# Two sets of heads in the first attention stage, and another order of ScalarE's and VectorE's work in the recurrent stage

## The chip, the cores and the metric

The kernel runs on one NeuronCore of a Trainium2 chip. Its engines are TensorE (PE in the profile; PEld is its weight load), VectorE (DVE), ScalarE (ACT), GpSimd (POOL) and SyncE (SP), which issues most of the transfers. The metric is the device time of one execution in microseconds; the time of a kernel is the median of its runs.

## The reference

Two blocks of two layers each run over one sequence of 256 tokens with 1024 channels, in fp32. The first block's layer 0 is a mixer of pooling and attention, its layer 1 a recurrent mixer, each followed by a convolutional feed-forward. The second block (three kinds of attention in each layer) is not touched by the change. Cut to what is:

```python
def pool_attn_mixer(h, w_in, pool_w, pool_scale, q_gain, k_gain, w_out):      # layer 0
    u, q, k, v = jnp.split(h @ w_in, [512, 1024, 1536], axis=-1)
    p = multiscale_pool_minus_identity(u)        # mean over 2, 4, 8, 16 tokens, less u, by 128 columns
    p = einsum('bsgc,gcd->bsgd', p.reshape(B, S, 4, 128), pool_w).reshape(B, S, 512) * pool_scale
    a = moba_attention(q, k, v, q_gain, k_gain)  # 8 heads of 64, head_rms on q and k, causal, slopes
    return jnp.concatenate([p, a], axis=-1) @ w_out

def rglru_mixer(h, w_in, conv_w, conv_b, w_a, b_a, w_x, b_x, lam, w_out):     # layer 1
    gate, xr = jnp.split(h @ w_in, 2, axis=-1)   # 1280 columns each
    xr = causal_dwconv(xr, conv_w, conv_b)       # 4 taps
    xb = xr.reshape(B, S, 10, 128)
    r = sigmoid(einsum('bsnc,ncd->bsnd', xb, w_a) + b_a)
    i = sigmoid(einsum('bsnc,ncd->bsnd', xb, w_x) + b_x)
    log_a = -8.0 * r * softplus(-lam)
    a, b = exp(log_a), sqrt(-expm1(2.0 * log_a)) * (i * xr)
    hs = associative_scan(combine, (a, b))       # h[t] = a[t] * h[t-1] + b[t]
    return (gelu(gate) * hs) @ w_out
```

## The kernel before

**Tiling.** Activations lie with channels on the partitions and the 256 tokens along the free axis. All weights come in units of 128 x 2048 floats (1 MB). SyncE transfers unit n into one of three `raw` slots as soon as unit n-3 is split. ScalarE's `split` copies it, rounded, to `w_hi` (L468), after waiting that unit n-3 has been used by TensorE; VectorE's `split` writes the rest, `raw - w_hi`, to `w_lo` (L937). TensorE multiplies each tile in three passes (`three`, L1595 to L1597: high x high, high x low, low x high), 48 matmuls to a unit. Each engine runs its own written list in order and waits on semaphores. `after(n)` on ScalarE and on VectorE does all splits up to unit n+3, so where it stands in an engine's list decides what waits behind a split.

**Stages.** `pa` (12 units, the pooling and attention mixer), `ffn0` (33), `rg` (15, the recurrent mixer), `ffn1`, then the second block. A stage's RMS norm is not applied ahead: the projection runs on x times gain, and VectorE multiplies the result by the reciprocal root (`scale`, L997).

**`pa`.** Units 0 to 3 are the columns of q and k (q heads 0-3, q heads 4-7, k heads 0-3, k heads 4-7), 4 and 5 are v, 6 and 7 are the pooling's u, 8 to 11 the output projection. ScalarE copies each q or k group (L615) and squares it (L617). When all four are there, `set_stat` sums squares by head on TensorE (L1775), ScalarE takes the root (L641), VectorE the reciprocal, `broadcast` spreads it over the partitions (L1798), and `head_norm` (L1165) scales q and k. `token_values` (L626) writes v. `attention` then runs 8 maps, one a head: scores on TensorE by twos (L1825), slope and row minimum on VectorE (L1180, L1182), exponentials on ScalarE (L671), a transpose on TensorE (L1844), its copy to `pt` on ScalarE (L650), the product with v on TensorE (L1866), and after each four heads the division on VectorE (`outputs`, L1199, L1210) and a transpose of that pair of tiles. Halves of units 6 and 7 are put between the maps 0 to 3 on TensorE (`half_units`). GpSimd's `pooling` starts when both u groups are out. After the attention TensorE applies the four pooling matrices (L1925), ScalarE scales the result (L732) and rounds it to `h_hi` (`to_h`, L715), GpSimd writes `h_lo` (L1519), and the four output units run.

**`rg`.** Five steps of 256 columns. Step k has a gate unit g, a branch unit x and an output unit o, in the order `RG_ORDER`. VectorE scales x's group, ScalarE applies bias and last tap (`branch`, L766), VectorE the other three taps (`conv`, L1323). TensorE's `gates` (L1967) multiplies with the two 128 x 128 block matrices, and waits for `conv`. ScalarE takes tanh of both (L781, L783), then exp (L788) and a second tanh (L790); VectorE combines them (L1332), squares the decay `qk[5]` (L1335) and uses it (L1336); ScalarE takes the root (L796), VectorE multiplies and scans along time (L1341, L1343), multiplies with the gelu of the gate (L1351) and rounds (L1356); GpSimd writes `y_lo`, and `second(k)`, the output unit, can run. At the stage's start `first_unit` (g0) is followed by `normed` (L1642), the sum of squares over channels.

Of the kernel before, what the change touches and what calls it, by code (L numbers as in the profile page):

```python
# [28 lines left out]
P = 128  # L29
S = 256  # L30
# [32 lines left out]

HY_STORED = {6: 8, 7: 11, 8: 12, 9: 9, 10: 10, 11: 6, 12: 7}
# [37 lines left out]
def build(nc, W, XT, CON, CON0, VEC, PW, RW, PE_T, POSR, POSC, LAM, OUT, stages=STAGES):  # L102
# [5 lines left out]
    with ExitStack() as ctx:  # L108
# [69 lines left out]
        def pair(t, j):  # L178
# [12 lines left out]
            rgelu rtx xcv rmm rsig rth rm rsb rgy ryhi ry_ready  # L191
# [46 lines left out]
        def stored(n):  # L238


            for a in ffs:
# [44 lines left out]
        def acc_free(eng, s, j, b):  # L286
# [18 lines left out]
            "pa": dict(groups=8, parts=0, pairs=4, sets=1, maps=8, ogroups=2, opairs=2),  # L305
# [11 lines left out]
        def spread_bank(s, k):  # L317


            return bank[2 + (total(s, "pairs") + k) % 4]  # L320
# [136 lines left out]
        def _(act):  # L457
# [228 lines left out]
            def attention(s, fillers):  # L686
# [22 lines left out]
                if kind(s) == "pa":  # L709
                    for u in uses(s, n):  # L710
                        turn(s, u)

# [4 lines left out]
            def pa(s):  # L717
                ub = B[s]
                norm(s)
                for e in range(4):  # L720
                    after(ub + e)
                    evacuate(s, e, pair(qk, e), set_slot(s, e))
                set_root(s, 0, 64, 4)
                for e in (4, 5):
                    after(ub + e)
                    token_values(s, e, 512 * (e - 4)).then_inc(sems["in_ev"], 1)
                attention(s, {1: ub + 6, 3: ub + 7})
                act.wait_ge(sems["vec_in"], 16)
                for j in range(2):
                    act.wait_ge(sems["pm_done"], j + 1)  # L730
                    for t in range(2):
                        last = nc.scalar.activation(hf[:, 2 * j + t], bank[j][:, t * S:(t + 1) * S], ACT.Copy,  # L732
                                                    scale=v_("pool_scale", 2 * j + t))
# [3 lines left out]
                for p in range(2):  # L737
                    act.wait_ge(sems["pt_ev"], use_no(s, ("pair", p)) + 1)
                    to_h(s, hf, 2 + p)
# [10 lines left out]
            def rg(s):  # L750
# [24 lines left out]
                for k in range(RG_STEPS):  # L775
                    hb = lambda t, c: rgh[:, 16 * k + 8 * t + c:16 * k + 8 * t + c + 1]
                    col = lambda v, t: v[:, 2 * k + t:2 * k + t + 1]

                    act.wait_ge(sems["rmm"], k + 1)
# [6 lines left out]
                    act.wait_ge(sems["rsig"], k + 1)  # L786
                    for t in range(2):
                        nc.scalar.activation(qk[:, 10 + t], qk[:, 4 + t], ACT.Exp, scale=col(cneg, t), bias=col(cneg, t))  # L788
                    for t in range(2):
                        last = nc.scalar.activation(qk[:, 8 + t], qk[:, 4 + t], ACT.Tanh, scale=col(cpos, t),  # L790
                                                    bias=col(cpos, t))
                    last.then_inc(sems["rth"], 1)
# [1506 lines left out]
```

## Time and profile before

| | us |
|---|---|
| median of 3 runs | 1630.66 |
| lowest and highest of them | 1629.74, 1633.18 |
| the profiled execution | 1629.44 |
| its span, first to last instruction | 1627.6 |
| TensorE busy | 1565.2 |
| VectorE busy | 1140.0 |
| ScalarE busy | 908.4 |
| GpSimd busy | 163.2 |

Busy time says how long an engine had an instruction under way; the waits of the engine that the end depends on are what a change of order can take away. Stage `pa` lies at 0 to 120 us of the span, `rg` at about 308 to 419 us. Every time below is in microseconds from the span's start. In a row, the bracket at the end is the idle time of that engine just before the row, and the instruction that ended it.

### The profile page before, as it was taken

How to read it: one execution, taken by the hardware profiler on the slowest of the kernel's cores; microseconds unless marked ns; L12 is line 12 of the kernel's file. 1: busy time of each engine (PE TensorE's matmuls, PEld its weight loads, DVE VectorE, ACT ScalarE, POOL GpSimd, SP SyncE). 2: the span in 40 equal slices, each digit the busy share in tenths (PEclk: the TensorE clock that was granted, in tenths of full speed). 3: DMA queues.
4: the chain of work that ended last, by engine and by line, in shares of the span. 5: the costliest groups of instructions: out<-in, count | busy, mean ns of one | idle time of the engine just before them, and what ended most of it. 6: DMA issues, size and time to landing. Idle time of an engine off the chain costs nothing.

```text
span 1627.6 us, 30223 instructions
## 1 busy us (share of the span) xinstructions
PE 1565.2 (96%) x12828; PEld 1510.4 (93%) x12828; DVE 1140.0 (70%) x1366; ACT 908.4 (56%) x1207; POOL 163.2 (10%) x94
## 2 busy tenths in 40 slices
PE   7889999989999999999999999998999999999998
PEld 7779999988999999788899999998889889999998
DVE  6637877877987787667547876568677647777566
ACT  6437554677656555545564744455645645655444
POOL 0121121101012110000022010010000012010010
PEclk9989999999999999999999999999999999999999
DMA  9334555534446545433335455545433334455552
GB/s 319 108 118 159 207 188 188 175 112 151 159 165 209 194 159 181 153 104 104 104 111 181 152 199 181 193 156 181 156 130 104 104 107 159 152 201 178 194 181 78
DMA packets 38268, 258.73 MB, mean 159 GB/s; under 512 B 4752, under 2 KB 5392, under 8 KB 7568
## 3 DMA queue, kind: packets, MB, share of 16 engines
q1 hardware_dynamic: 37728, 255.33, 45.6%
q10 hardware_dynamic: 432, 1.84, 0.3%
q8 instruction: 83, 1.36, 0.3%
q14 instruction: 25, 0.20, 0.0%
HBM read 256.10 MB, written 1.05 MB: 158 GB/s over the span
## 4 chain that ended last, share of the span: by engine, by line
PE 73%; issue 10%; ACT 8%; DVE 7%; POOL 1%; DMA 1%; SPq 0%; ACTq 0%; POOLq 0%; DVEq 0%
PE bank L1595 22%; PE bank L1597 21%; PE bank L1596 21%; ACT w_hi L468 3%; DVE w_lo L937 3%; PE bank L1866 3%; PE bank L1825 2%; PE bank L1844 2%; PE bank L1775 1%; DVE qk L1323 1%; PE bank L1798 1%; DMA raw<-W 1%; PE bank L1967 1%; POOL y_lo L1519 1%; DVE h_lo L952 1%
## 5 line engine op out<-in xcount | busy, mean ns | idle before, releaser
L1595 PE MATMUL bank<-h_hi,w_hi 128*128 128x256 f32 x2640 | 753.1, 285 | 22.9 <-DVE h_lo L952 14.7
L1597 PE MATMUL bank<-h_hi,w_lo 128*128 128x256 f32 x2640 | 742.5, 281 | 0.0
L1596 PE MATMUL bank<-h_lo,w_hi 128*128 128x256 f32 x2640 | 742.5, 281 | 0.0
L937 DVE TENSOR_TENSOR w_lo<-raw,w_hi 128x2048 fp32r<-128x2048 f32 x238 | 553.9, 2329 | 202.2 <-ACT w_hi L468 201.3
L468 ACT ACTIVATE w_hi<-raw 128x2048 fp32r<-128x2048 f32 x238 | 454.9, 1912 | 276.1 <-PE bank L1597 274.4
L1595 PEld LDWEIGHTS bank<-h_hi,w_hi 128*128 128x128 f32 x2640 | 499.2, 189 | 37.1 <-issue 13.6
L1597 PEld LDWEIGHTS bank<-h_hi,w_lo 128*128 128x128 f32 x2640 | 501.7, 190 | 0.0
L1596 PEld LDWEIGHTS bank<-h_lo,w_hi 128*128 128x128 f32 x2640 | 498.8, 189 | 0.4
L1595 PE MATMUL bank<-y_hi,w_hi 128*128 128x256 f32 x1040 | 295.2, 284 | 4.0 <-POOL y_lo L1519 2.2
L1597 PE MATMUL bank<-y_hi,w_lo 128*128 128x256 f32 x1040 | 291.9, 281 | 0.0
L1596 PE MATMUL bank<-y_lo,w_hi 128*128 128x256 f32 x1040 | 291.9, 281 | 0.0
L1595 PEld LDWEIGHTS bank<-y_hi,w_hi 128*128 128x128 f32 x1040 | 195.9, 188 | 7.9 <-issue 3.0
L1597 PEld LDWEIGHTS bank<-y_hi,w_lo 128*128 128x128 f32 x1040 | 197.1, 190 | 0.0
L1596 PEld LDWEIGHTS bank<-y_lo,w_hi 128*128 128x128 f32 x1040 | 195.7, 188 | 0.2
L1519 POOL TENSOR_TENSOR y_lo<-qk,y_hi 128x512 fp32r<-128x512 f32 x53 | 112.4, 2122 | 812.1 <-ACT y_hi L578 698.1
L1041 DVE SCALAR_TENSOR_TENSOR qk<-bank,vec,qk 128x255 f32<-128x255 f32 (+1 forms) x264 | 115.0, 477 | 41.1 <-ACT qk L552 32.7
L997 DVE TENSOR_TENSOR bank<-bank,rinv_t 128x512 f32<-128x512 f32 (+1 forms) x123 | 84.9, 691 | 33.2 <-PE bank L1597 32.4
L552 ACT ACTIVATE qk<-bank,vec 128x256 f32<-128x256 f32 x88 | 44.7, 558 | 103.8 <-DVE bank L997 103.7
L1866 PE MATMUL bank<-val,pt 128*128 128x64 f32 (+1 forms) x448 | 59.3, 276 | 5.7 <-ACT pt L650 5.4
L1866 PEld LDWEIGHTS bank<-val,pt 128*128 128x128 f32 x448 | 56.0, 195 | 7.9 <-ACT pt L650 7.3
L578 ACT ACTIVATE y_hi<-qk 128x512 fp32r<-128x512 f32 x44 | 27.5, 624 | 62.4 <-PE bank L1597 59.3
L567 ACT ACTIVATE qk<-qk 128x512 f32<-128x512 f32 x44 | 27.9, 633 | 60.5 <-DVE qk L1041 60.1
(219 smaller groups left out, 1332.1 us busy)
## 6 DMA issues: line engine op xcount, KB each, us to landing
raw<-W SPq DMA_DIRECT2D x238, 1024.0 KB, 4.8
wide<-RW ACTq DMA_DIRECT2D x1, 1280.0 KB, 7.3
raw<-W SPq DMA_DIRECT2D x2, 512.0 KB, 5.5
x<-XT SPq DMA_DIRECT2D x4, 256.0 KB, 6.7
OUT<-x SPq DMA_DIRECT2D x4, 256.0 KB, 2.0
wide<-CON SPq DMA_DIRECT2D x1, 768.0 KB, 9.1
val<-PE_T ACTq DMA_DIRECT2D x2, 256.0 KB, 2.6
vec<-VEC SPq DMA_DIRECT2D x1, 390.0 KB, 4.8
```

Of the source, the lines that this page charges most:

```text
L468: nc.scalar.activation(w_hi[:, n0 % NW], raw[:, n0 % NRAW], ACT.Copy).then_inc(sems["hi_done"], 1)
L552: ins = nc.scalar.activation(T[:, t], up[:, t * S:(t + 1) * S], ACT.Identity, bias=b, scale=w)
L937: V.tensor_tensor(w_lo[:, n0 % NW], raw[:, n0 % NRAW], w_hi[:, n0 % NW].bitcast(F32), ALU.subtract)\
L997: return V.tensor_tensor(z, z, rinv.unsqueeze(1).broadcast_to([P, w // S, S]), ALU.mult)\
L1041: return V.scalar_tensor_tensor(out=dst, in0=src, scalar=w, in1=dst, op0=ALU.mult, op1=ALU.add)
L1519: return G.tensor_tensor(dst, src, hi.bitcast(F32), ALU.subtract)
L1595: T.matmul(out, w[0], a[0], start=start, stop=False, **kw)
L1596: T.matmul(out, w[0], a[1], start=False, stop=False, **kw)
L1597: return T.matmul(out, w[1], a[0], start=False, stop=stop, **kw)
L1825: last = T.matmul(b[:, qt * S:(qt + 1) * S], qk[p:p + w, tq, qt * P:(qt + 1) * P], qk[p:p + w, tk], start=a == 0, stop=a == n - 1)
L1844: m = T.transpose(b[:, kt * S + qt * P:kt * S + qt * P + P], src[:, qt * S + kt * P:qt * S + kt * P + P], c_("ident"))
L1866: last = T.matmul(o, pt[:, i % 2, kt * S + qt * P:kt * S + qt * P + P], value(m["v"], kt), start=kt == 0, stop=kt == 1)
```

## The change

In `pa` the units come in the order q heads 0-3, k heads 0-3, q heads 4-7, k heads 4-7, v heads 0-3, u first half, v heads 4-7, u second half (`PA_ORDER`), and the output units in the order 2, 0, 1, 3. The head norm is done in two sets of four heads: statistics of set 0 stand between units 2 and 3 on TensorE, its spread behind unit 3, the statistics of set 1 in the middle of unit 4, its spread behind the first half of unit 5. Scores of heads 0 and 1 follow unit 4. Halves of units 5, 6 and 7 lie between maps 0 to 5. The second v group is written by VectorE. Pooling runs in two halves, each as soon as its u group is there. The pooling matrices and the transpose of the last pair stand in the middle of the first output unit, and the `h_lo` of the stage is written by VectorE in place of GpSimd.

In `rg` the first branch unit starts ahead of `normed`; the splits of a step stand ahead of its tanh on ScalarE and ahead of its combination on VectorE; `branch` and `conv` of the next step stand ahead of root and scan (in step 2 the branch stands between scan and output); the square of the decays is ScalarE's; exp of step k waits until step k-1's scan has been used; the last `y_lo` is VectorE's; and the split of unit o3 on VectorE moves from behind step 3 to behind the last step's combination.

```diff
+PA_ORDER = (0, 2, 1, 3, 4, 6, 5, 7, 10, 8, 9, 11)
@@ ScalarE, pa
-                for e in range(4):
+                for e, t in ((0, 0), (1, 2)):
                     after(ub + e)
-                    evacuate(s, e, pair(qk, e), set_slot(s, e))
-                set_root(s, 0, 64, 4)
-                for e in (4, 5):
-                    after(ub + e)
-                    token_values(s, e, 512 * (e - 4)).then_inc(sems["in_ev"], 1)
-                attention(s, {1: ub + 6, 3: ub + 7})
+                    evacuate(s, e, pair(qk, t), set_slot(s, e))
+                set_root(s, 0, 64, 2)
+                after(ub + 2)
+                evacuate(s, 2, pair(qk, 1), set_slot(s, 2))
+                evacuate(s, 3, pair(qk, 3), set_slot(s, 3))
+                after(ub + 3)
+                set_root(s, 1, 64, 4)
+                token_values(s, 4, 0).then_inc(sems["in_ev"], 1)
+                after(ub + 4)
+                attention(s, {1: ub + 5, 3: ub + 6, 5: ub + 7})
@@ ScalarE, rg
+                    after(at(RG_FILL[k]))
+
                     act.wait_ge(sems["rmm"], k + 1)
...
                     act.wait_ge(sems["rsig"], k + 1)
+                    if k:
+
+                        act.wait_ge(sems["rgy"], k)
...
-                    last.then_inc(sems["rth"], 1)
-                    after(at(RG_FILL[k]))
+                        nc.scalar.activation(qk[:, 8 + t], qk[:, 4 + t], ACT.Tanh, scale=col(cpos, t), bias=col(cpos, t))
+                    act.wait_ge(sems["rexp"], k + 1)
+                    nc.scalar.activation(pair(qk, 6), pair(qk, 5), ACT.Square).then_inc(sems["rth"], 1)
+                    if k in (0, 1, 3):
+
+                        branch(k + 1)
@@ VectorE, pa
+                scale_group(s, 2)
                 set_scale(s, 0)
-                for k in range(4):
-                    head_norm(s, k, (2 * k, 2 * k + 1), (v_("pa_gain", 2 * k), v_("pa_gain", 2 * k + 1)))
-                after(ub + 5)
+                after(ub + 2)
+                scale_group(s, 3)
+                pg = lambda t: v_("pa_gain", t)
+                head_norm(s, 0, (0, 1), (pg(0), pg(1)))
+                head_norm(s, 1, (4, 5), (pg(4), pg(5)))
+                set_scale(s, 1)
+                after(ub + 3)
@@ VectorE, rg
                     dve.wait_ge(sems["rth"], k + 1)
-                    link(V.tensor_tensor(pair(qk, 6), pair(qk, 5), pair(qk, 5), ALU.mult))
...
                 for k in range(RG_STEPS):
+                    if k + 1 < RG_STEPS:
+                        after(at(RG_FILL[k]))
                     gates(k)
-                    after(at(RG_FILL[k]))
...
+                    elif k + 1 < RG_STEPS:
                         branch(k + 1)
                         conv(k + 1)
-                    elif k + 1 < RG_STEPS:
-                        branch(k + 1)
                         scan(k)
-                        conv(k + 1)
                         out(k)
                         gate((2, 3, None, 4)[k])
                     else:
+
+                        after(at("x4"))
                         scan(k)
                         out(k)
+                        last_low()
                         after(at("o3"))
-                    if k + 1 < RG_STEPS:
+                    if k + 2 < RG_STEPS:
                         after(at(f"x{k + 1}"))
@@ TensorE, pa
+                attention(s, fill)
+
+                def pooled():
...
+                for n, j in enumerate((2, 0, 1, 3)):
+                    pe.wait_ge(sems["h2_ready"], 4 * atts.index(s) + n + 1)
+                    onto(s, 0, ub + 8 + n, h_parts(j), n == 0, n == 3, between=None if n else pooled)
```

TensorE at the end of the attention in `pa`, before: the transposes of map 7 and of the last pair (`ot`), the pooling matrices (`wide`) and the first output unit (`h_hi,w_hi`).

```order
L1844 MATMUL bank6<-con,lg 128x128 [waits exp_done,pt_ev]
L1844 MATMUL bank6<-con,lg 128x128 x3
L1866 MATMUL bank3<-val,pt 128x64 [waits pt_ev]
L1866 MATMUL bank3<-val,pt 128x64 x3
L1844 MATMUL bank7<-con,ot 128x128 [waits o_ev,pt_ev]
L1844 MATMUL bank7<-con,ot 128x128 x3
L1925 MATMUL bank0<-wide 128x256 [waits pool_in,pool_p]
L1925 MATMUL bank0<-wide 128x256
L1925 MATMUL bank1<-wide 128x256 x2
L1595 MATMUL bank0<-h_hi,w_hi 128x256 [waits lo_done,h2_ready,psc]
```

The same place in the changed kernel:

```order
L1901 MATMUL bank6<-con,lg 128x128 [waits exp_done,pt_ev]
L1901 MATMUL bank6<-con,lg 128x128 x3
L1929 MATMUL bank3<-val,pt 128x64 [waits pt_ev]
L1929 MATMUL bank3<-val,pt 128x64 x3
L1649 MATMUL bank0<-h_hi,w_hi 128x256 [waits lo_done,h2_ready,in_ev]
```

The output unit follows the last map at once; the transpose of the pair and the pooling matrices stand 24 matmuls further on.

ScalarE in step 0 of `rg`, before: tanh from banks 6 and 7, exp and tanh with scales from `geo`, a split (`w_hi`), root, then `branch` from bank 5.

```order
L781 ACTIVATE qk<-bank6,geo 128x256 [waits rmm,rgc_ready]
L781 ACTIVATE qk<-bank6,geo 128x256
L783 ACTIVATE qk<-bank7,geo 128x256 x2
L788 ACT_TABLE_LOAD
L788 ACTIVATE qk<-qk,geo 128x256 [waits rsig]
L788 ACTIVATE qk<-qk,geo 128x256
L790 ACTIVATE qk<-qk,geo 128x256 x2
L468 ACTIVATE w_hi<-raw 128x2048 [waits w_used,raw_in2]
L796 ACT_TABLE_LOAD
L796 ACTIVATE qk<-qk 128x512 [waits rm]
L766 ACTIVATE qk<-bank5,vec 128x256 [waits scaled]
```

And in the changed kernel:

```order
L472 ACTIVATE w_hi<-raw 128x2048 [waits w_used,raw_in2,rgc_ready]
L790 ACTIVATE qk<-bank6,geo 128x256 [waits rmm]
L790 ACTIVATE qk<-bank6,geo 128x256
L792 ACTIVATE qk<-bank7,geo 128x256 x2
L800 ACT_TABLE_LOAD
L800 ACTIVATE qk<-qk,geo 128x256 [waits rsig]
L800 ACTIVATE qk<-qk,geo 128x256
L804 ACTIVATE qk<-qk,geo 128x256 x2
L806 ACTIVATE qk<-qk 128x512 [waits rexp]
L773 ACTIVATE qk<-bank5,vec 128x256 [waits scaled]
L773 ACTIVATE qk<-bank5,vec 128x256
L812 ACT_TABLE_LOAD
```

The split stands ahead of tanh, the square (L806) is new, and `branch` stands ahead of the root.

VectorE in the last step of `rg`, before: the gate of step 4, a split (`w_lo`, unit o3), the three instructions of the combination, a split (unit o4), the scan.

```order
L1311 TENSOR_TENSOR qk<-bank4,rinv_t 128x512 [waits w_used]
L937 TENSOR_TENSOR w_lo<-raw,w_hi 128x2048 [waits hi_done]
L1332 SCALAR_TENSOR_TENSOR qk<-qk 128x512 [waits rsig]
L1335 TENSOR_TENSOR qk<-qk 128x512 [waits rth,dve_chain]
L1336 SCALAR_TENSOR_TENSOR qk<-qk 128x512 [waits dve_chain]
L937 TENSOR_TENSOR w_lo<-raw,w_hi 128x2048 [waits hi_done]
L1341 TENSOR_TENSOR qk<-qk 128x512 [waits rsb]
L1343 SCALAR_TENSOR_TENSOR qk<-qk 128x256 [waits dve_chain]
```

And in the changed kernel:

```order
L1353 TENSOR_TENSOR qk<-bank4,rinv_t 128x512 [waits w_used]
L1374 SCALAR_TENSOR_TENSOR qk<-qk 128x512 [waits rsig]
L1377 SCALAR_TENSOR_TENSOR qk<-qk 128x512 [waits rth,dve_chain]
L953 TENSOR_TENSOR w_lo<-raw,w_hi 128x2048 [waits hi_done]
L1382 TENSOR_TENSOR qk<-qk 128x512 [waits rsb]
L1384 SCALAR_TENSOR_TENSOR qk<-qk 128x256 [waits dve_chain]
```

The split between combination and scan is now that of unit o3; the split of o4 stands behind the last `y_lo`.

## Rows read from the trace of the kernel before

**Rows 1.** The page: busy time of TensorE.

```profile
PE 1565.2 (96%) x12828; PEld 1510.4 (93%) x12828; DVE 1140.0 (70%) x1366; ACT 908.4 (56%) x1207; POOL 163.2 (10%) x94
```

**Rows 2.** Waits of TensorE, 0 to 125 us: total, times, longest.

```profile
PE bank L1866 <- ACT pt L650: 2.9, 4, 1.3
PE bank L1825 <- ACT val L626: 2.9, 1, 2.9
```

**Rows 3.** TensorE by stretches: length, busy (instructions), granted clock, DMA share, GB/s.

```profile
55.62:58.26 2.64, 2.64 (x12) 0.50 0.60 133
75.25:84.10 8.85, 5.78 (x45) 1.00 0.16 44
84.10:97.67 13.57, 9.55 (x37) 0.62 0.11 48
97.67:120.30 22.63, 22.63 (x191) 1.00 0.39 133
345.60:358.30 12.70, 12.70 (x97) 0.88 0.39 124
```

**Rows 4.** TensorE in order of time, stage pa: start, duration, instruction, count.

```profile
25.61 0.37 PE L1595 MATMUL bank<-h_hi,w_hi 128*128 128x256 f32 x1
...
60.29 1.13 PE L1825 MATMUL bank<-qk 64*128 64x256 f32 x8
...
64.29 1.00 PE L1866 MATMUL bank<-val,pt 128*128 128x64 f32 x8
65.13 0.61 PE L1844 MATMUL bank<-con,lg 128*128 128x128 f32 x4
```

**Rows 5.** ScalarE and VectorE in order of time, stage pa.

```profile
32.13 0.59 ACT L617 ACTIVATE sq<-bank 128x512 f32<-128x512 f32 x1
...
31.76 2.29 DVE L937 TENSOR_TENSOR w_lo<-raw,w_hi 128x2048 fp32r<-128x2048 f32 x1 [0.16 <-ACT w_hi L468]
...
45.55 3.22 DVE L1165 SCALAR_TENSOR_TENSOR qk<-qk,vec,bank 128x256 f32<-128x256 f32 x8 [1.69 <-PE bank L1798]
...
90.94 0.76 DVE L1210 TENSOR_TENSOR ot<-bank,rec 128x256 f32<-128x256 f32 x2
```

**Rows 6.** Waits of TensorE, 300 to 425 us: total, times, longest.

```profile
PE bank L1967 <- DVE qk L1323: 9.0, 4, 3.1
PE bank L1642 <- DVE sq L984: 1.2, 1, 1.2
```

**Rows 7.** TensorE in order of time, stage rg: the gates of steps 0, 1 and 4.

```profile
327.40 1.89 PE L1967 MATMUL bank<-qk,wide 128*128 128x256 f32 x8
...
343.76 2.45 PE L1967 MATMUL bank<-qk,wide 128*128 128x256 f32 x8 [3.10 <-DVE qk L1323]
...
398.53 2.61 PE L1967 MATMUL bank<-qk,wide 128*128 128x256 f32 x8 [2.12 <-DVE qk L1323]
```

**Rows 8.** ScalarE in order of time, step 0 of stage rg.

```profile
329.39 0.84 ACT L781 ACTIVATE qk<-bank,geo 128x256 f32<-128x256 f32 x2 [3.77 <-PE bank L1967]
...
330.97 1.28 ACT L788 ACT_TABLE_LOAD   x1
...
333.27 1.08 ACT L790 ACTIVATE qk<-qk,geo 128x256 f32<-128x256 f32 x2
334.25 1.90 ACT L468 ACTIVATE w_hi<-raw 128x2048 fp32r<-128x2048 f32 x1
...
337.47 0.63 ACT L796 ACTIVATE qk<-qk 128x512 f32<-128x512 f32 x1
339.12 1.02 ACT L766 ACTIVATE qk<-bank,vec 128x256 f32<-128x256 f32 x2 [1.02 <-DVE bank L997]
```

**Rows 9.** VectorE in order of time, steps 0 and 1 of stage rg.

```profile
335.18 0.69 DVE L1336 SCALAR_TENSOR_TENSOR qk<-qk 128x512 f32<-128x512 f32 x1
...
339.71 1.27 DVE L1343 TENSOR_TENSOR_SCAN qk<-qk 128x256 f32<-128x256 f32 x2
341.02 2.69 DVE L1323 SCALAR_TENSOR_TENSOR qk<-bank,vec,qk 128x255 f32<-128x255 f32 x6
```

More of the change, by code:

```diff
@@ L238, in stored @@
         def stored(n):
+            if "pa" in used and B["pa"] <= n < B["pa"] + UNITS["pa"]:
+                return first + B["pa"] + PA_ORDER[n - B["pa"]]
             for a in ffs:
@@ L304, in build @@
         PLAN = {
-            "pa": dict(groups=8, parts=0, pairs=4, sets=1, maps=8, ogroups=2, opairs=2),
+            "pa": dict(groups=8, parts=0, pairs=4, sets=2, maps=8, ogroups=2, opairs=2),
             "hy": dict(groups=30, parts=5, pairs=13, sets=3, maps=24, ogroups=8, opairs=6)}
@@ L736, in pa @@
                     to_h(s, hf, j)
-                for p in range(2):
-                    act.wait_ge(sems["pt_ev"], use_no(s, ("pair", p)) + 1)
-                    to_h(s, hf, 2 + p)
+                act.wait_ge(sems["pt_ev"], use_no(s, ("pair", 1)) + 1)
+                to_h(s, hf, 3)
                 for n in range(8, 11):
@@ L1851, in outputs @@
                 g = total(s, "ogroups") + m["g"]
+                if kind(s) == "pa" and i == 0:
+                    pe.wait_ge(sems["qk_done"], total(s, "pairs") + 4)
+                if kind(s) == "pa" and i == 4:
+                    pe.wait_ge(sems["in_ev"], total(s, "groups") + 7)
                 if kind(s) == "hy" and i == 0:
@@ L1906, in pa @@
                 normed(s)
-                for e in range(2, 4):
-                    feature_unit(s, ub + e, e)
+                feature_unit(s, ub + 2, 2)
+                pe.wait_ge(sems["picked"], 1)
+                set_stat(s, 0, 0, [two(0), two(4)], 1)
+                feature_unit(s, ub + 3, 3)
+                pe.wait_ge(sems["spread_in"], 12 * 16)
+                broadcast(s, 0, 0, [(0, 2), (4, 2)])
                 unit(ub + 4)
@@ L1918, in pa @@
-                pe.wait_ge(sems["qk_done"], total(s, "pairs") + 4)
-                pe.wait_ge(sems["in_ev"], total(s, "groups") + 6)
-                attention(s, half_units(s, ub + 6, 6, 2))
-                pe.wait_ge(sems["pool_p"], 1)
-                pe.wait_ge(sems["pool_in"], 16)
-                for g in range(4):
-                    m = T.matmul(bank[g // 2][:, (g % 2) * S:(g % 2 + 1) * S],
-                                 wide[:, 13:15].rearrange("p a n -> p (a n)")[:, g * P:(g + 1) * P], pool_u[:, g, 8:8 + S],
-                                 start=True, stop=True)
-                    if g % 2:
-                        m.then_inc(sems["pm_done"], 1)
@@ new lines, in pa @@
+                attention(s, fill)
+                def pooled():
+                    pe.wait_ge(sems["o_ev"], total(s, "opairs") + 2)
+                    transposed(s, ("pair", 1))
+                    pe.wait_ge(sems["lp_done"], total(s, "maps") + 8)
+                    pe.wait_ge(sems["pool_p"], 1)
+                    pe.wait_ge(sems["pool_in"], 16)
+                    for g in range(4):
+                        m = T.matmul(bank[4 + g // 2][:, (g % 2) * S:(g % 2 + 1) * S],
+                                     wide[:, 13:15].rearrange("p a n -> p (a n)")[:, g * P:(g + 1) * P], pool_u[:, g, 8:8 + S],
+                                     start=True, stop=True)
+                        if g % 2:
+                            m.then_inc(sems["pm_done"], 1)
```

114 lines of the change are left out of this document (78 added, 36 removed).

## The prediction

> **What bounds the kernel.** I read the page's busy times first, then TensorE's waits by stage, then the engines in order of time around the longest waits. TensorE is busy for 96% of the span [rows 1]. Its work is the same after the change but for one more start of each statistics group, so only its waits, and the stretches in which its granted clock is low, can be won. In stage pa the waits are one of 2.9 us ahead of the scores, four for the copies to `pt` [rows 2], and the tail of the attention, where TensorE idles 8.85 - 5.78 = 3.1 us and then 13.57 - 9.55 = 4.0 us, the second stretch at a mean clock of 0.62 [rows 3]. In stage rg it waits four times for the taps, 9.0 us in all, and once 1.2 us for the sum of squares [rows 6]; after the first of these the clock is 0.88 over two units [rows 3]. A unit takes 22.63 / 4 = 5.7 us at the high level [rows 3], half a unit 2.85.
>
> **Stage pa, first half.** Unit 2 starts at 25.61 [rows 4] and ends at 31.3. The statistics of set 0 now stand right behind it and need the square of group 1, which ends at 32.13 + 0.59 = 32.7 [rows 5]: a new wait of 1.5. From there TensorE runs 0.5 of statistics, unit 3, 0.5 of spread (to 39.7), unit 4 with 0.5 of statistics inside, and is at the scores at 45.9. VectorE's scaling of group 3, four head norms (half of 3.2 us for eight, [rows 5]) and a second reciprocal fit beside unit 4, so the scores don't wait: 2.9 gone. What is late next is the first transpose. VectorE has the split of unit 6 ahead of the logits; 2.3 for the split [rows 5], two instructions of 0.7 like those in [rows 9], then the exponentials behind a split and a table load on ScalarE bring it to 51.2, where TensorE has been free since 50.35: a wait of 0.85. The 2.9 wait was followed by a low clock that I put at 1.4 to 1.8 by a half unit of 24 matmuls (some 14 of them 0.10 longer, the difference of the two levels in [rows 3], and the scores); that goes with it. First half: -2.9 - 1.6 + 1.5 + 0.85 = -2.1.
>
> **Stage pa, tail.** Six half units now cover maps 0 to 5 where four covered 0 to 3. Scores take 1.06, a product 0.84, a transpose 0.45, by the distances of starts and the durations less their overlap [rows 4]. With these TensorE goes without a wait from 51.2 to the end of the transposes behind unit 7 at about 76. Then ScalarE has a split of 1.9 [rows 8] ahead of the copy of map 5, since that split waits for unit 7 to be used: 0.8 of waiting. The last maps are a chain through ScalarE as before: waits of about 0.7, 0.8, 0.2 and 0.8. The last product ends at 83.3, then reciprocal, division (0.76, [rows 5]) and the subtraction for the first `h_lo`, 0.69 as for any two-input pass of 512 [rows 9], lie on the path because VectorE's list has the division first: 1.8 to 2.0 of waiting, and the output units start at 85.0 instead of 97.67 [rows 3]. Pooling in halves ends on GpSimd near 84 and isn't waited for. The transpose of the pair and the pooling matrices (0.5 + 1.6 at the high clock) now lie inside the first output unit, and their copies, roundings and subtractions (about 3 us through ScalarE and VectorE) are covered by its second half of 2.85. I add 0.9, because half units between maps take 2.94 and not 2.85 (4.00 from 60.29 to 64.29 less 1.06) and a waited-for group ends some 0.1 later. So 85.0 + 22.6 + 2.1 + 0.9 = 110.6 without any low clock, against 120.3 [rows 3]. The waits from 76 to 85 sum to 5.1 in 9 us, against 3.1 in 8.85 us that were followed by the 0.62 stretch. So I count on a low clock again, over three to five short groups and the first matmuls of the output units: 1.7 to 3.9, take 2.8. Stage pa ends at 113.4: **-6.9** (-5 to -10).
>
> **Stage rg, start.** The sum of squares waits 1.2 less, but stands behind half a unit more. From it, root, reciprocal, gate, split, scale, `branch` and `conv` take 10.9 us to the first gates, and TensorE has only 2.85 + 5.7 to do meanwhile. The gates of step 0 come at 327.8 against 327.40 [rows 7]: +0.4, two waits (0.5 and 1.0) for one.
>
> **Stage rg, steps.** Before, from tanh at 329.39 the chain ran tanh, load, exp, tanh, then square, combination, split, scale, product, scan (1.27) and at last taps, which end at 343.71 [rows 8, 9]: 14.3. Now: the second tanh starts 3.88 after the first [rows 8], the square 1.0 later for 0.6, combination and scale 1.35 by two steps of 0.61 and a latency, `branch` 1.02 [rows 8], taps 2.69 [rows 9]: 10.7. VectorE loses 0.69 and ScalarE gains 0.6 for the square; one handover is neither gained nor lost. The gates of step 1 then need only the gate unit in front, 340.8 against 343.76 [rows 7]. But ScalarE's own round is now a bound: tanh to square 5.5, wait 1.4, `branch` 1.0, load 1.28 and root 0.6, load and gelu 1.9, two splits 3.8 = 15.5, against 13.0 of TensorE's work in a step with two units. So tanh of step 1 starts at 345.3, of step 2 at 360.8, step 3 at 377.7, though TensorE is ready 2.5, 2.8 and 1.0 earlier. Adding 10.7, the gates start at 340.8, 355.9, 374.8 and 388.4 (steps 1 to 4; step 3 is held by root and scan of step 2, which stand ahead of that branch). TensorE waits 2.2 at step 2, 0.2 at step 3, 0.7 for the split of x4 (now behind the taps), nothing at step 4: before, the last gates came at 398.53 [rows 7], so **-10.1** to that point.
>
> **Stage rg, end.** Here a wait comes back. The split of o3 on VectorE stands behind the last combination. ScalarE does the split of o4, a load (1.28) and then tanh at 392.5; square and combination end at 397.4, the split at 399.65. TensorE has done gates and o2 at 395.6: a wait of **4.05** ahead of o3. Queued behind it is only o4, for which `y` is ready at 403.5 and the split at 405.7. So o3 and o4 end at 411.05 at the high clock, 419.3 before. A wait of 4.05 is longer than that of 3.10 [rows 7] after which 12.70 us passed for 11.4 of work plus 0.5 in the gates [rows 3]: I add 2.0. The 2.2 wait may cost as much, but most of it is swallowed by the 4.05; 0.6 for it. The first unit of ffn1 waits some 0.3 more for its splits. 411.05 + 2.0 + 0.6 + 0.3 = 414.0: **-5.3** (-2 to -8).
>
> **Sum.** -6.9 - 5.3 = -12.2 on 1629.44, 1617.2; the median stood 1.2 above that execution: **1618**. The later stages are the same, but wherever the clock is about to fall or rise there, 2 us may come or go.
>
> **A rule of the Trainium skill against this.** In this trace a table load lasts 1.28 and the next function starts 0.02 behind it; the load at 330.97 is one [rows 8]. The Trainium skill ("ScalarE: Activation LUTs", What ACT_TABLE_LOAD costs) counts a drain of about 1.38 us to each switch, 2.66 in all. By that rule ScalarE's round would have three switches of 1.38 more, and since the changed order makes that round the bound, an estimate by that page would take 12 us back over three rounds, 1630. The row shows no such drain, so the sum keeps 1.28.
>
> **Rivals.** (1) Forecast, 1612 to 1624: **66%**. (2) The waits I see coming back don't: the tail of pa keeps the high clock (-2.8), and the o3 wait with its low clock is short because ScalarE reaches tanh earlier (-4 to -6). For: three of the waits rest on splits placed by a few tenths. Against: the order lists fix o3 behind the combination. 1618 - 8 = 1610; **14%** for 1605 to 1612. (3) Only one stage pays: ScalarE's round slips further (exp now waits for the last output of the step before, splits wait for units), each round 1.7 longer, and rg gives nothing: 1624 to 1627.4; **12%**. (4) No change, within 0.2%: rounds 4 us longer in rg, as if each table switch drained: 1630; **4%**. (5) Slower: TensorE stays at the low level through the four output units of pa because the short waits from 76 to 85 are closer together. At a granted clock of 0.50, the 1.2 GHz level, a matmul takes 2.64 / 12 = 0.22, the first stretch of [rows 3], instead of 0.12; 192 of them cost 19.2 more, 1618 + 19.2 - 2.8 = 1634.4, and with o3 and o4 low too, 96 x 0.10 = 9.6 less the 2.0 counted, 1642. It is slower by over 0.2% from about 190 low matmuls on, o3 and o4 among them; before, the high level was back for the whole of the output units [rows 3]. **4%**.
>
> The time is the forecast's. Low 1609 takes in most of rival 2, high 1625 some of rival 3. A measurement can tell about 0.2%, 3.3 us, from no change: faster 92%, within 4%, slower 4%.
>
> **What would show it.** The scores start near 46 and the output units of pa near 85; gates of step 4 near 388; a wait of about 4 for `w_lo` ahead of the o3 unit, the longest of rg; ScalarE's tanh of steps 1 and 2 starting right behind a split, not behind TensorE. Wrong would be: gates waiting over 3 us for the taps, or no wait at o3.

## The result, and the profile after

| | before | after |
|---|---|---|
| median, us | 1630.66 | 1618.79 |
| lowest and highest, us | 1629.74, 1633.18 (5 runs) | 1614.69, 1622.99 (5 runs) |
| the profiled execution, its span | 1629.44, 1627.6 | 1618.79, 1617.0 |

The ratio is 0.9925, with a 95% interval of 0.9909 to 0.9942. The prediction was 1618.0. Measured a second time, beside eleven runs of the kernel before, the changed kernel had a median of 1616.30 us (1613.03 to 1621.55, 6 runs) against 1629.84: 0.9922, interval 0.9905 to 0.9939.

The page of after answers to [rows 1]: TensorE's busy time hardly moves, and the span gets 10.6 us shorter.

```profile
PE 1563.3 (97%) x12828; PEld 1509.5 (93%) x12828; DVE 1140.0 (71%) x1369; ACT 909.9 (56%) x1211; POOL 157.5 (10%) x91
```

TensorE's waits, 0 to 125 us, and then 300 to 425 us, in after (total, times, longest), answer to [rows 2] and [rows 6]:

```profile
PE bank L1649 <- DVE h_lo L968: 11.1, 2, 9.8
PE bank L1929 <- ACT pt L654: 2.2, 3, 0.8
PE bank L1649 <- issue: 1.7, 1, 1.7
PE bank L1829 <- ACT sq L621: 1.3, 1, 1.3
...
PE bank L1649 <- DVE w_lo L953: 3.5, 1, 3.5
PE bank L2058 <- DVE qk L1365: 2.6, 2, 1.9
PE bank L1649 <- DVE h_lo L968: 1.3, 1, 1.3
```

The 9.8 us are the start of the kernel. The 2.9 us ahead of the scores are gone, and 1.3 for the first set's statistics and 1.7 ahead of the output units have come. The 9.0 us for the taps have become 2.6, and 3.5 ahead of one `w_lo` have come. In order of time, TensorE in after (start, duration, instruction, count, and the wait ahead in the bracket), first stage `pa`, then the gates, o3 and the next feed-forward stage's start in `rg`:

```profile
32.21 1.06 PE L1829 MATMUL bank<-sq,con 128*32 128x256 f32 x8 [1.32 <-ACT sq L621]
39.08 1.13 PE L1852 MATMUL bank<-crs,con 32*128 32x256 f32 x8
43.17 1.06 PE L1829 MATMUL bank<-sq,con 128*32 128x256 f32 x8
47.24 1.13 PE L1882 MATMUL bank<-qk 64*128 64x256 f32 x8
...
88.83 0.55 PE L1649 MATMUL bank<-h_hi,w_hi 128*128 128x256 f32 x1 [1.73 <-issue]
...
116.47 0.36 PE L1649 MATMUL bank<-h_hi,w_hi 128*128 128x256 f32 x1 [1.26 <-DVE h_lo L968]
...
337.90 1.89 PE L2058 MATMUL bank<-qk,wide 128*128 128x256 f32 x8
353.05 2.44 PE L2058 MATMUL bank<-qk,wide 128*128 128x256 f32 x8 [1.89 <-DVE qk L1365]
...
386.57 1.89 PE L2058 MATMUL bank<-qk,wide 128*128 128x256 f32 x8
397.69 0.35 PE L1649 MATMUL bank<-y_hi,w_hi 128*128 128x256 f32 x1 [3.54 <-DVE w_lo L953]
...
412.08 0.35 PE L1649 MATMUL bank<-h_hi,w_hi 128*128 128x256 f32 x1 [1.26 <-DVE h_lo L968]
```

The places to compare are the starts of the first feed-forward stage and of the second. Before, they lie at 121.89 and 420.42. One table of TensorE over three stretches tells how the time between was won: unit 2 of `pa` to the first feed-forward unit, 160 us inside the first feed-forward stage, and the gates of step 0 to the next feed-forward stage. The columns are the stretch, its length, TensorE busy (instructions), granted clock, DMA share, GB/s. Before:

```profile
25.61:121.89 96.28, 84.76 (x658) 0.93 0.42 146
130.00:290.00 160.00, 159.78 (x1380) 1.00 0.56 191
327.40:420.42 93.02, 83.02 (x619) 0.94 0.40 139
```

After:

```profile
24.96:116.47 91.51, 84.55 (x658) 0.94 0.44 153
130.00:290.00 160.00, 159.43 (x1350) 1.00 0.54 184
325.00:412.08 87.08, 80.38 (x617) 0.96 0.41 150
```

Length less busy is waiting. In `pa` it falls from 11.5 to 7.0 us and the busy part stays: 4.8 us in length, and unit 2 itself began 0.65 earlier, so the stage ends 5.4 earlier. (The 0.65 is not the change's: `low_first` below, with the same start, has unit 2 at 25.74.) In `rg` waiting falls from 10.0 to 6.7, and the busy part from 83.0 to 80.4 for the same matmuls: 5.9 us. Before has three stretches of 3.4 us at the 1.2 GHz level there and after two. There a matmul takes 0.215 us from start to start and not 0.117, so the third stretch was worth at most 1.7 of the 2.6 us. Most of the other 0.9 goes with the waits themselves: the first matmul of the gates behind a wait takes 0.32 us to the next one instead of 0.22, and the last one ahead of a wait counts as busy to its end. Between the two lies what nobody forecast: in the same 160 us after starts 1350 matmuls where before starts 1380, at the same granted clock of 1.00. Over the whole stretch from 121.89 to 327.40 and from 116.47 to 325.00 that is 205.5 us against 208.5, and 3.0 us of the gain were given back there. From the second feed-forward stage on, 2.3 us more were won, in a part that the change doesn't touch: -5.4 + 3.0 - 5.9 - 2.3 = -10.6. Before spends 3.4 us more at the 1.2 GHz level there, worth up to 1.7 of the 2.3.

### The profile page after: what moved, and what is told of

Its sections match the earlier page's. It is cut to its first block, busy times and chain, and to the rows that moved or that the text cites. A ratio compares the mean times of both kernels' runs of the same rounds, so it can differ in the third digit from the quotient of the medians.

```text
span 1617.0 us, 30230 instructions
## 1 busy us (share of the span) xinstructions
PE 1563.3 (97%) x12828; PEld 1509.5 (93%) x12828; DVE 1140.0 (71%) x1369; ACT 909.9 (56%) x1211; POOL 157.5 (10%) x91
## 4 chain that ended last, share of the span: by engine, by line
PE 75%; issue 12%; ACT 7%; DVE 5%; POOL 1%; DMA 1%; SPq 0%; POOLq 0%; ACTq 0%; DVEq 0%
PE bank L1649 22%; PE bank L1650 21%; PE bank L1651 21%; ACT w_hi L472 3%; PE bank L1882 2%; PE bank L1929 2%; PE bank L1901 2%; DVE w_lo L953 2%; PE bank L1829 1%; PE bank L1852 1%; DVE rinv_t L1007 1%; DMA raw<-W 1%; POOL y_lo L1571 1%; DVE bank L1013 0%; ACT h_hi L492 0%
## 5 line engine op out<-in xcount | busy, mean ns | idle before, releaser
L571 ACT ACTIVATE qk<-qk 128x512 f32<-128x512 f32 x44 | 27.9, 633 | 60.5 <-DVE qk L1065 60.1
```

## Experiments: the two halves apart

The theory was that two separate gains add up; the rival, that `rg` gains only because `pa` ends earlier. The first kernel has `pa` of after with `rg` of before, the second the reverse. Of the one block that both stages share on GpSimd, each took its own line:

```diff
 # pa_only
-                    for q in range(RG_STEPS - 1):
+                    for q in range(RG_STEPS):
 # rg_only
+                    to_h(s, hf)
```

> The attention stage of the changed kernel with the recurrent stage of the kernel before. Theory (two separate gains): the first feed-forward unit starts 5.4 us earlier than in the kernel before (116.47 against 121.89, as in the trace after), the recurrent stage keeps the length of the kernel before, from the start of its last covered feed-forward units to the start of the next feed-forward stage 8.34 - 2.24 = 6.1 us longer than in the changed kernel; time 1630.7 - 5.4 = 1625 us, and up to 3.6 us more or less by the pace that the matmul stream takes in the first feed-forward stage (0.1156 or 0.1183 us a matmul, 1344 of them). Rival (the recurrent stage gains only because the stage before it ends earlier and its loads come earlier): its waits of 9.0 us at one line shrink here too, time near 1620.

> The attention stage of the kernel before with the recurrent stage of the changed kernel. Theory: the recurrent stage is 6.1 us shorter than in the kernel before, the attention stage unchanged (first feed-forward unit near 121.9); time 1630.7 - 6.1 = 1624.5 us, up to 3.6 us more or less by the pace of the stream in the first feed-forward stage. If the two halves of the change are independent, the two gains add up to the 11.9 us between the medians within that pace term. Rival (the gain of the recurrent stage depends on the other half): less than 4 us shorter.

Measured, ten runs of each beside nineteen of the kernel before (median 1629.97): `pa_only` 1626.10 us, ratio 0.9986 (0.9963 to 1.0008), so its gain is not clear of the spread by time alone; `rg_only` 1623.64, ratio 0.9961 (0.9937 to 0.9985). The two gains add up to 3.9 + 6.3 = 10.2 us, against 11.9 between the medians at first. The times alone don't settle it: the runs of the kernel before reach from 1620.34 to 1638.46 there. The positions in the trace do. The first feed-forward unit starts at 116.97 in `pa_only` and 121.47 in `rg_only`. From the gates of step 0 to the second feed-forward stage, `pa_only`:

```profile
325.93:420.07 94.14, 84.03 (x619) 0.93 0.40 138
```

and `rg_only`:

```profile
326.80:412.68 85.88, 79.17 (x616) 0.98 0.42 152
```

Beside 93.02 before and 87.08 after, each half has its own effect and none of the other's: -4.9 for `pa`, -7.1 for `rg` here. The rival is out. `pa_only` has 3.4 us more at the 1.2 GHz level than before in this stretch, and is 1.1 longer. Five traces have this same `rg` in full, and they show what one trace can say: 87.08 (after), 85.86 (`after_again`), 85.88 (`rg_only`), 85.88 (`stat_mid`), 87.01 (`low_first`). The 1.2 us of after are one stretch at the 1.2 GHz level behind the gates of step 2, which the four others don't show; `low_first` ran twice as long at that level around the start of o3.

## Experiments: what in stage rg gains

Three parts of the change were undone one at a time in the changed kernel. First the splits, behind the gates again on both engines:

```diff
 # ScalarE
-                    after(at(RG_FILL[k]))
-
                     act.wait_ge(sems["rmm"], k + 1)
...
                     nc.scalar.activation(pair(qk, 6), pair(qk, 5), ACT.Square).then_inc(sems["rth"], 1)
+                    after(at(RG_FILL[k]))
 # VectorE
-                    if k + 1 < RG_STEPS:
-                        after(at(RG_FILL[k]))
                     gates(k)
+                    if k + 1 < RG_STEPS:
+                        after(at(RG_FILL[k]))
```

> The changed kernel with another part undone: the splits of a step stand behind its gates again, on ScalarE (3.7 us for two) and on VectorE (5.2 us for two). Theory (the splits inside the chain from tanh to taps were what the waits of 9.0, 4 and 3.1 us of the kernel before came from): the stage gets 5 to 8 us longer than in the changed kernel, with the waits ahead of the gates back at the taps. Rival (ScalarE's round of 15.3 us bounds, wherever the splits stand in it): less than 2 us.

Then the order of the taps:

```diff
 # VectorE
-                        conv(k + 1)
                         scan(k)
+                        conv(k + 1)
                         out(k)
 # VectorE, step 2: branch and conv behind out and the split of o0
 # ScalarE: branch(k + 1) behind the root, in every step
-                    if k in (0, 1, 3):
-
-                        branch(k + 1)
```

> The changed kernel with one part undone: the taps of the next branch behind the scan on VectorE again, and ScalarE's first tap behind the root. Theory by the trace after: in step 0 the taps end 1.4 us later (gates of step 1 about 1.2 later), but ScalarE's round gets 1.3 us shorter, since it no longer waits for VectorE's scaling of the branch ahead of the root, and VectorE's two splits bound the next step: gates of step 2 within 0.5 us of the changed kernel; stage 0 to 2 us longer. Rival (the prediction's view, the chain from tanh to taps of 10.7 against 14.3 us carries the gain): 3 to 6 us longer.

Then the squares of the decays:

```diff
 # VectorE
+                    link(V.tensor_tensor(pair(qk, 6), pair(qk, 5), pair(qk, 5), ALU.mult))
 # ScalarE
-                    nc.scalar.activation(pair(qk, 6), pair(qk, 5), ACT.Square).then_inc(sems["rth"], 1)
```

> The changed kernel with its third part undone: the squares of the decays on VectorE (0.69 us) instead of ScalarE (0.62 us). Theory: the square lies between the second tanh and the gate's product on either engine, so a step changes by 0.1 us; from the first to the last gates within 0.6 us of the 60.4 to 61.6 us that the traces with the square on ScalarE have. Rival (VectorE or ScalarE is full at that point, and the move of 0.6 us counts in every step): 2 to 3 us longer.

The same stretch, gates of step 0 to the second feed-forward stage, in `splits_behind`:

```profile
322.77:416.38 93.61, 83.22 (x616) 0.95 0.39 137
```

in `taps_behind`:

```profile
325.95:410.96 85.01, 78.60 (x617) 1.00 0.42 149
```

in `square_dve`:

```profile
327.15:413.49 86.34, 79.11 (x616) 0.98 0.42 151
```

and in a second trace of the changed kernel itself, `after_again`. It lacks the low stretch of step 2, as `taps_behind` and `square_dve` do, and is the one to compare with:

```profile
322.68:408.54 85.86, 79.09 (x617) 0.98 0.42 152
```

With the splits behind the gates everything is lost: 93.6 us, 0.6 longer than before the change. Undoing the squares costs 0.5 us, less than the traces of one kernel differ by. The order of the taps bought nothing here: undone, the stretch is 0.85 **shorter**, where I expected 0 to 2 us longer. Each of these is one trace; single runs took 1624.08 us (`splits_behind`) and 1615.40 (`taps_behind`) beside 1632.97 for the kernel before, and 1617.74 (`square_dve`) beside 1635.72. The other parts of the change in `rg` (x0 ahead of `normed`, the last `y_lo` on VectorE) were not undone by themselves. My forecast had priced the chain of 10.7 against 14.3 us as one piece, splits and taps together. Two engines in `taps_behind` show what each part does, ScalarE in step 0 and the start of step 1, then VectorE's taps:

```profile
327.95 0.84 ACT L790 ACTIVATE qk<-bank,geo 128x256 f32<-128x256 f32 x2 [0.70 <-PE bank L2054]
...
334.75 0.63 ACT L808 ACTIVATE qk<-qk 128x512 f32<-128x512 f32 x1
335.29 1.00 ACT L773 ACTIVATE qk<-bank,vec 128x256 f32<-128x256 f32 x2
...
342.21 0.84 ACT L790 ACTIVATE qk<-bank,geo 128x256 f32<-128x256 f32 x2 [0.37 <-PE bank L2054]
...
337.44 2.68 DVE L1361 SCALAR_TENSOR_TENSOR qk<-bank,vec,qk 128x255 f32<-128x255 f32 x6
```

and the same of after:

```profile
327.00 0.84 ACT L790 ACTIVATE qk<-bank,geo 128x256 f32<-128x256 f32 x2 [0.69 <-PE bank L2058]
...
333.93 1.02 ACT L773 ACTIVATE qk<-bank,vec 128x256 f32<-128x256 f32 x2 [1.45 <-DVE bank L1013]
...
342.34 0.82 ACT L790 ACTIVATE qk<-bank,geo 128x256 f32<-128x256 f32 x2
...
334.98 2.69 DVE L1365 SCALAR_TENSOR_TENSOR qk<-bank,vec,qk 128x255 f32<-128x255 f32 x6 [1.09 <-ACT qk L773]
```

From tanh to the taps' end the changed kernel needs 337.67 - 327.00 = 10.7 us and `taps_behind` 340.12 - 327.95 = 12.2, so the splits, with the square, take 2.1 us out of the 14.3 and the taps' place 1.5. But in the changed kernel ScalarE idles 1.45 us, waiting for VectorE's scale ahead of the first tap, with the root queued behind; its round is 15.3 us and the next tanh starts with no wait, right behind a split. With the taps behind, the first tap follows the root without that wait, and the round is 14.3, ended by TensorE. Over the first two steps the two are 0.5 us apart. The later steps do cost `taps_behind` more, 62.7 us from first to last gates against 60.5 in `after_again`. That is then taken back ahead of o3, where both wait for the same split on VectorE: 1.71 us there, 3.55 in `after_again`. No low clock follows the 1.71, and one stretch follows the 3.55.

That wait was tried next: in the changed kernel VectorE makes the low half of o3, or of o3 and o4, ahead of the last gates.

```diff
-                    if k + 1 < RG_STEPS:
-                        after(at(RG_FILL[k]))
+                    after(at(RG_FILL[k]) if k + 1 < RG_STEPS else at("x4"))   # o3_early; at("g4") in o34_early
                     gates(k)
...
-                        after(at("x4"))
                         scan(k)
```

> Recurrent stage of the changed kernel, but VectorE makes the low half of unit o3 ahead of the last step's gates, in its idle time of 2.0 us there (389.9 to 391.9). Theory (the 3.54 us wait ahead of o3 is that split, and o4's is the next thing late): o3 starts without a wait near 394.2 instead of 397.7; o4's split still stands behind the last combination and its low half, done near 402.6, so a new wait of about 2.5 us appears ahead of o4; start of the next feed-forward stage 1.5 to 2 us earlier than 412.1 (counted from the same start of the stage). Rival (full gain): no wait ahead of o4, 4 us earlier. Second rival: the last step's gates slip by the split, and nothing is gained.

> As o3_early, but the low halves of both o3 and o4 stand ahead of the last step's gates on VectorE. The two splits take 4.5 us of which 2.0 were idle; the first gate operation slips by 2.4 us, but the second waits for ScalarE's square until 394.65 anyway and slips by 0.3. Theory: no wait ahead of o3, at most 0.5 us ahead of o4 (for the last product's low half, near 400.3), no low-clock stretch there; next feed-forward stage 4 to 5 us earlier than in the changed kernel. Rival: the slip of the gates passes down the chain in full (2.4 us), o4 waits 2.5 us, gain 2 us or less.

> Both splits of o3 and o4 ahead of the last gates on VectorE (as in the run o34_early), and the taps behind the scan again (as in taps_behind). In the changed kernel the later gates of taps_behind (62.7 us from first to last gates against 60.4) were taken back by a shorter wait ahead of o3 (1.71 against 3.54 us). Theory (the taps' order counts only once the wait ahead of o3 no longer hides it): first gates to the next feed-forward stage 81.8 + 2.3 = about 84 us. Rival (the order of the taps is worth nothing in any case): 81.8 to 82.3.

The same stretch, in `o3_early`:

```profile
325.68:409.15 83.47, 77.75 (x616) 1.00 0.42 153
```

in `o34_early`:

```profile
324.23:406.03 81.80, 77.79 (x616) 1.00 0.43 159
```

in `o34_taps_behind`:

```profile
325.74:408.79 83.05, 77.87 (x617) 1.00 0.44 157
```

and VectorE in order of time ahead of the last gates' products in `o34_early`:

```profile
387.88 5.21 DVE L953 TENSOR_TENSOR w_lo<-raw,w_hi 128x2048 fp32r<-128x2048 f32 x2
393.01 0.68 DVE L1374 SCALAR_TENSOR_TENSOR qk<-qk 128x512 f32<-128x512 f32 x1
393.72 0.69 DVE L1377 SCALAR_TENSOR_TENSOR qk<-qk 128x512 f32<-128x512 f32 x1
```

Both splits early are worth 4.1 us beside `after_again`, 5.3 beside the first trace of after: 2.8 us of waiting (6.8 to 4.0) and the rest in the busy part (79.1 to 77.8), which has no stretch at the low level any more. One split moved gives 2.4 beside `after_again` and 3.6 beside after, where I expected 1.5 to 2; a wait of 2.95 comes ahead of o4, where I expected 2.5, but no low clock follows it, and that is what the expectation left out. The theory sized o4's wait in `o34_early` at 0.5 at most and it is 1.2: the two splits took 5.2 us and not 4.5, so the gates' second product came 1.0 us later and not 0.3, and the root 0.5. The first of the two took 3.0 us and not 2.3, with a `y_lo` on GpSimd in its first 0.8 us; the same split takes 3.0 beside a `y_lo` in `o3_early` (389.32) and in after (341.28). Now that nothing hides it, the order of the taps counts: 83.05 - 81.80 = 1.25 us, where I expected 2.3. So the same edit is worth -0.85 or +1.25, by what stands ahead of o3, one trace on each side.

## Experiments: the two new waits of stage pa

```diff
 # low_first, VectorE: ahead of the division of the last group
+                            if kind(s) == "pa" and e == n - 1:
+                                pair_low(s, 0, 2)
                             outputs(s, ended(s, e))
 ...
 # stat_mid, TensorE
-                set_stat(s, 0, 0, [two(0), two(4)], 1)
-                feature_unit(s, ub + 3, 3)
+                unit(ub + 3)
+                b = group_bank(s, 3)
+                column_tile(ub + 3, 0, b[:, 0:S])
+                set_stat(s, 0, 0, [two(0), two(4)], 1)
+                column_tile(ub + 3, 1, b[:, S:2 * S]).then_inc(sems["w_used"], 1)
```

> Attention stage of the changed kernel, but VectorE makes the low half of the first output block (0.68 us, its inputs are there at 85.6) ahead of the division of the last group (0.20 + 0.76 us) instead of behind it. Theory (the 1.73 us wait ahead of the four output units is that order on VectorE): the output units start right behind the last product, 1.7 us earlier; counted from the last product's start to the first feed-forward unit 1.7 us shorter than the 31.34 us of the changed kernel (85.13 to 116.47). Rival: the transposes and pooled matmuls inside the first output unit, which need the division, now wait; gain below 0.5.

> Attention stage of the changed kernel, but the statistics of the first set of heads stand in the middle of unit 3 instead of ahead of it. Theory (the 1.32 us wait is for ScalarE's squares of unit 2, and half a unit covers it): no wait there, and no wait ahead of the spread behind unit 3 or at most 0.5; scores and all that follows 0.8 to 1.3 us earlier, counted from the start of unit 2. Rival (the chain statistics, root, reciprocal, spread, norm, scores is what bounds, and it now begins later): the wait comes back at the spread or ahead of the scores, gain under 0.3, or a loss of up to 1.5.

> The changed kernel with three edits together: the splits of o3 and o4 ahead of the last gates on VectorE, the low half of the first output block ahead of the division, the statistics in the middle of unit 3. Theory: the stretch from the first gates to the next feed-forward stage is 81.8 us (87.1 in the changed kernel), the attention stage 1.7 + 1.0 us shorter; 8 us less than the changed kernel of the same chip, near 1611 us, with runs spread by some 14 us in steps of 3.6 us, one for each of the four feed-forward stages that takes the slower pace. Rival (the spread comes from elsewhere): the runs lie within 0.3% of their median.

> The changed kernel itself, beside the one with three edits and the kernel before on one chip. Theory: ratio to before 0.9925 as first measured, within its interval (11 us: 5.4 from the attention stage, 5.9 from the recurrent stage, less 3.2 where its first feed-forward stage took the slower pace, which must not happen in every run, so possibly up to 13). Rival: the first measurement drew lucky paces, ratio above 0.995.

From unit 2 to the first feed-forward unit, in `low_first`:

```profile
25.74:114.81 89.07, 83.86 (x659) 0.96 0.45 156
```

in `stat_mid`:

```profile
24.93:116.36 91.43, 85.80 (x658) 0.93 0.45 153
```

in `after_again`:

```profile
25.25:116.97 91.72, 84.75 (x659) 0.94 0.44 153
```

and in `best`:

```profile
25.59:110.94 85.35, 81.26 (x659) 1.00 0.47 165
```

Waiting falls from 7.0 us in `after_again` to 5.2 with the low half first and to 5.6 with the statistics in the middle. Both waits go in full and come back nowhere. From the last product to the first feed-forward unit `low_first` takes 29.8 us, against 31.3 after: 1.5 of the 1.7 expected. In `stat_mid` the scores start 45.82 - 24.93 = 20.9 us behind unit 2, against 22.3 after, a little more than the 0.8 to 1.3 expected. But `stat_mid` is only 0.3 us shorter, for its tail ran at the low level 3.4 us longer. The four rows differ by 4.5 us in the busy part for the same matmuls, and `best`, whose tail never fell, shows the price: at most 84.75 - 81.26 = 3.5 us for the 10.2 us at the low level in `after_again` (at most, since `best` has two waits less there, and these leave the busy part a little too). With the same edits apart it fell in every trace, so I don't claim that they prevent it together. No run undoes a part of the first change in `pa` by itself; that its 4.8 us come from the 2.9 ahead of the scores and from the covered maps is read from the waits alone.

`best` has these two edits and that of `o34_early`. Five runs gave 1608.19 us (1605.62 to 1611.88), ratio to before 0.9868 (0.9849 to 0.9886): 8.1 us less than the changed kernel measured beside it, as expected. Its `rg` stretch was 82.66, against 81.8 expected. The spread that I expected of its runs, 14 us, was 6.3, within 0.3% of the median to either side, so on `best` the rival's expectation held; the spread shows in other runs (below).

## Why the prediction was right, and where it wasn't

The time was right within 0.8 us. Part of that is luck: -6.9 - 5.3 had to become -5.4, +3.0, -5.9 and -2.3.

**Stage pa, first half.** Unit 2 to scores was to take 20.3 us and took 22.3. The failed step is a term: I wrote 0.5 us for a group of eight short matmuls, twice for statistics and once for the spread. From start to start they take 33.20 - 32.21 = 0.99 and 40.14 - 39.08 = 1.06. The halves of unit 4 took 3.0 to 3.1 and not 2.85. The new wait was 1.32 against 1.5, and the one of 0.85 ahead of the first transpose never came: TensorE was late itself.

**Stage pa, tail.** The chain through ScalarE waited 0.82, 0.45, 0.69 and 0.69 us against 0.8, 0.7, 0.2 and 0.8, and the wait behind VectorE's division was 1.73 against 1.8 to 2.0; `low_first` shows its cause. The pooled matmuls lay inside the first output unit as said. The low clock came and cost some 3.3 (84.55 - 81.26, at most) against 2.8. Output units started at 88.83 against 85.0: 1.3 was there at the scores, 0.7 came by the transposes behind unit 7 (77.9 against 76), and 1.9 in the last maps, where the clock fell at 81.4. In `o34_early`, where it fell only at 87.4, the same maps took 78.6 to 87.5, 8.9 us, as the 9.0 in the forecast. So the order was right there; the sum added the whole low clock only behind the 85.0.

**Stage rg, steps.** Counted from the gates of step 0, I had those of steps 1 to 4 at 13.0, 28.1, 47.0 and 60.6 us. After has them at 12.9, 28.1, 48.5 and 61.6, the extra low stretch among it, `after_again` at 13.2, 28.1, 46.7 and 60.5. ScalarE's round was 15.3 against 15.5. A table load in it lasts 1.28 us and the next function follows 0.02 behind, as in [rows 8]:

```profile
328.58 1.28 ACT L800 ACT_TABLE_LOAD   x1
329.88 1.09 ACT L800 ACTIVATE qk<-qk,geo 128x256 f32<-128x256 f32 x2
```

These rows show no drain, and rival 4, rounds 4 us longer, is out. The Trainium skill ("ScalarE: Activation LUTs", What ACT_TABLE_LOAD costs) counts a drain of about 1.38 us to each switch of function set, by an estimate from that figure 4.1 us for the three of a round; this trace does not agree, and the measurement decides.

What was wrong here is the account of what buys what, and not the number. The chain came out at the 10.7 us of the forecast (whose listed terms add up to 10.5), but the sum took it as one piece and ScalarE's round as its given limit. The round is that long **because of** the taps' order, which puts ScalarE's wait for VectorE's scale ahead of the root: 15.3 us against 14.3 without it. So the order takes 1.5 us out of the chain and puts 1.0 into the round. The splits ahead of the gates carry the gain, 7.8 us beside `after_again`.

**Stage rg, end.** The wait ahead of o3 was 3.54 against 4.05, by the split named. The low clock behind it cost 1.5 us and not 2.0: from o3 to the second feed-forward stage 14.3 to 14.4 us with it, 12.9 without it in `taps_behind`. (In `low_first`, twice as long at that level, it was 15.5.)

**Nowhere in it:** the pace of the stream in the feed-forward stage, +3.0. The forecast allowed for 2 us in the later stages, by the clock alone.

## What to carry to other kernels

In a step that passes between two engines, take out of the chain first what merely stands in it (here splits of later weights), then ask of every operation moved ahead what it now waits for and what is queued behind it. Price an edit together with the next wait: the taps' order gave -0.85 or +1.25 us as the wait ahead of o3 did or did not cover it. And count a removed wait with the low clock that may follow it: in `rg` one such stretch of 3.4 us fell away, up to 1.7 of the 5.9 us.

## What the runs showed of the hardware

**Two paces at the high level.** With no wait, at a granted clock of 1.00, the stream of 128x256 matmuls runs at one of two paces. In 80 us of the second and 100 us of the last feed-forward stage, in `pa_only`:

```profile
520.00:600.00 80.00, 80.00 (x694) 1.00 0.54 184
1450.00:1550.00 100.00, 100.00 (x868) 1.00 0.56 190
```

and in after:

```profile
520.00:600.00 80.00, 79.96 (x675) 1.00 0.52 177
1450.00:1550.00 100.00, 100.00 (x848) 1.00 0.53 185
```

The mean distance of starts is 0.1156 us or 0.1183 us. In each of the four feed-forward stages one of the two holds without a break over a long stretch, the same in all fourteen traces: 26, 17, 31 and 30 units of 48 matmuls. At 2.7 ns a matmul that is 3.4, 2.2, 4.0 and 3.9 us between the two paces (the 1344 matmuls of the expectations above were too many for the first two). Of these 56 stretches 10 ran at the quick pace. The stretch from the first feed-forward unit to the gates of step 0 took 205.3 to 205.7 us in five of the fourteen traces (before, `rg_only`, `splits_behind`, `after_again`, `best`) and 208.5 to 209.0 in the other nine, six of which have the code of `after_again` up to there. So it isn't the kernel's code alone that picks it. Nor is it the chip: on one chip, with the same code up to there, `splits_behind` took 205.7 and `taps_behind`, `o3_early` and `o34_early` 208.9. The time from the second feed-forward stage to the end, the same code everywhere, reached from 1196.1 us (`pa_only`, two stages at the quick pace) to 1207.2 (before). Together with the low stretches it can account for runs of one kernel 8 to 18 us apart, and it is why positions in the trace were compared here and not single times. What sets the pace stays open; I did not try to steer it.

**How often the low level follows a wait.** All six waits of 3.5 to 3.9 us ahead of o3 had one at their end or just behind it. The wait of 2.95 us ahead of o4 in `o3_early` had none. Of the waits of 1.6 to 2.1 us ahead of the gates of step 2 some were followed by one (after, `best`: 1.89 us) and some not (`square_dve`: 2.06). The tail of `pa`, with the same waits in it, had 3.4 us of it in `o34_early`, 10.2 in seven traces and 13.7 in `square_dve` and `stat_mid`; `low_first` and `best`, without the wait ahead of the output units, had 6.8 and none.
